# Reordering the transfers and sums where an MLP kernel turns from its up to its down projection

## The reference, cut to what matters

```python
    hm = _rms(x, norm_mlp) @ w_up
    x = x + jnp.square(jax.nn.relu(hm)) @ w_down
...
    y_prompt = _rms(xp, norm_final)
```

## Time and profile before

| | |
|---|---|
| median of 3 runs | 2661.9 us |
| profiled execution, device time | 2661.59 us |
| its span, first to last instruction | 2659.9 us |
| TensorE busy | 2617.6 us, 98% |
| VectorE busy | 1775.3 us, 67% |
| ScalarE busy | 1017.1 us, 38% |
| POOL busy | 148.0 us, 6% |
| mean granted clock of the TensorE | 0.996 of full |
| moved by DMA | 486.32 MB, mean 183 GB/s |
| time for the turn | about 1934 to 2030 us |

### The profile page before, as it was taken

One profiled execution on the slowest core, in us unless ns is written; L12 is line 12 of the kernel. 1 busy time (PEld: TensorE's weight loads), 2 busy tenths in 40 slices (PEclk: granted clock), 3 DMA queues, 4 the chain that ended last, 5 costly groups with the idle time before them and its releaser, 6 DMA issues.

```text
span 2659.9 us, 48846 instructions
## 1 busy us (share of the span) xinstructions
PE 2617.6 (98%) x20436; PEld 2564.5 (96%) x20436; DVE 1775.3 (67%) x2172; ACT 1017.1 (38%) x1317; POOL 148.0 (6%) x235
## 2 busy tenths in 40 slices
PE   8999999999999999999999999999999999999997
PEld 8989999999999998979999999999999999999997
DVE  7656533343443234257988888888887888888888
ACT  6532211111231122133566556555543333333344
POOL 1100000000000001000011110000010000000000
PEclk9999999999999999999999999999999999999998
DMA  8663222222223436433477777666688666566653
GB/s 284 226 219 99 92 87 89 87 88 87 90 82 125 171 111 251 175 145 132 135 247 242 248 252 237 215 239 220 220 301 305 231 223 207 203 218 235 219 168 107
DMA packets 142666, 486.32 MB, mean 183 GB/s; under 512 B 12672, under 2 KB 18944, under 8 KB 131232
## 3 DMA queue, kind: packets, MB, share of 16 engines
q1 hardware_dynamic: 105616, 293.08, 33.2%
q0 software_dynamic: 36880, 190.79, 19.5%
HBM read 402.96 MB, written 80.86 MB: 182 GB/s over the span
## 4 chain that ended last, share of the span: by engine, by line
PE 94%; DVE 2%; DMA 2%; ACT 1%; issue 1%; SPq 0%; DVEq 0%; ACTq 0%
PE psum_main L1731 39%; PE psum_main L2092 27%; PE psum_side L2092 20%; PE psum_main L1838 3%; DMA unit_raw<-weights 1%; PE psum_main L1946 1%; PE psum_main L2018 1%; PE psum_side L1911 1%; DVE unit_low L1405 1%; PE psum_side L1987 1%; DMA residual<-residual_kept 0%; DMA mem_raw<-mem_t 0%; ACT unit_high L846 0%; DVE residual L1697 0%; PE psum_side L1998 0%
## 5 line engine op out<-in xcount | busy, mean ns | idle before, releaser
L846 ACT ACTIVATE unit_high<-unit_raw 128x1024 fp32r<-128x1024 f32 x384 | 402.3, 1055 | 536.2 <-PE psum_main L2092 155.4
L1731 PE MATMUL psum_main<-inner_a,unit_high 128*128 128x272 f32 x3584 | 599.4, 289 | 0.0
L1405 DVE TENSOR_TENSOR unit_low<-unit_raw,unit_high 128x1024 fp32r<-128x1024 f32 x384 | 469.0, 1222 | 109.1 <-ACT unit_high L846 109.0
L643 ACT ACTIVATE unit_high<-unit_raw 128x1024 fp32r<-128x1024 f32 x226 | 239.2, 1059 | 717.6 <-PE psum_main L1731 662.3
L1731 PEld LDWEIGHTS psum_main<-inner_a,unit_high 128*128 128x128 f32 x3584 | 507.2, 188 | 3.1 <-issue 2.9
L1005 DVE TENSOR_TENSOR unit_low<-unit_raw,unit_high 128x1024 fp32r<-128x1024 f32 x226 | 276.2, 1224 | 234.5 <-ACT unit_high L643 231.8
L2092 PE MATMUL psum_main<-hidden,unit_high 128*128 128x272 f32 x2048 | 391.9, 290 | 6.1 <-DVE residual L1572 3.2
L2092 PE MATMUL psum_main<-tokens,unit_high 128*128 128x272 f32 x2048 | 388.5, 288 | 3.3 <-DVE hidden L1542 2.3
L1731 PE MATMUL psum_main<-inner_a,unit_low 128*128 128x272 f32 x1792 | 370.0, 287 | 0.0
L2092 PEld LDWEIGHTS psum_main<-hidden,unit_high 128*128 128x128 f32 x2048 | 324.7, 190 | 6.9 <-DVE residual L1572 3.8
L2092 PEld LDWEIGHTS psum_main<-tokens,unit_high 128*128 128x128 f32 x2048 | 321.8, 189 | 4.2 <-DVE hidden L1542 2.9
(11 more groups left out here) (232 smaller groups left out, 3366.7 us busy)
## 6 DMA issues: line engine op xcount, KB each, us to landing
unit_raw<-weights SPq DMA_DIRECT2D x482, 512.0 KB, 4.1
hidden<-hidden_kept POOLq DMA_DIRECT2D x56, 1088.0 KB, 6.5
hidden_kept<-hidden_staged POOLq DMA_DIRECT2D x31, 1904.0 KB, 7.5
unit_sum<-weights SPq DMA_DIRECT2D x63, 512.0 KB, 3.8
residual_kept<-residual POOLq DMA_DIRECT2D x32, 272.0 KB, 5.4
cache_ring_t<-cache_k POOLq DMA_DIRECT2D x8, 1024.0 KB, 8.2
cache_low_a<-cache_v POOLq DMA_DIRECT2D x8, 1024.0 KB, 10.9
cache_ring_a<-cache_k POOLq DMA_DIRECT2D x8, 1024.0 KB, 7.8
```

The costliest lines, as they stand in the source:

```text
L643: act.activation(WHI[:, s, :], RAW[:, s, :], ACT.Copy).then_inc(high_ready, 1)
L846: act.activation(WHI[:, slot, :], raw, ACT.Copy).then_inc(mlp_high, 1)
L1405: dve.tensor_tensor(WLO[:, slot, :], raw, WHI[:, slot, :].bitcast(F32), ALU.subtract) \
L1731: ins = pe.matmul(out, weights_at(w), moving, start=first and n == 0, stop=last and n == len(passes) - 1)
```

## The change

Three edits, all at the turn. On POOL, the load of hidden block 2 (i == 2, and so all behind it) also waits for `mlp_high` 225, which is the high part of w11 of quad 32. On POOL too, the store of quad 30, the wait for its landing and piece 2 of the residual now stand ahead of the wait for `stage_ready` 64 and piece 1. For quads 33 to 36 (`crowded`), SP loads w11 first, behind its wait for `sum_4` of the quad before, and then w22 and w21, both behind the wait for the fifth low part; w12 and the second w22 follow as before. On the DVE, `sum_1` of these quads stands behind `add_down` of product 4 and the first low part, instead of ahead of them.

```diff
--- before.py
+++ after.py
@@ -410,6 +410,8 @@
             def into(q, tile):
                 return tile if q < QUADS else tile.rearrange("p (u n) -> p u n", u=2)
 
+            crowded = range(QUADS + 1, QUADS + 5)
+
 
             for q in range(2 * QUADS):
                 w11, w12, w21, w22 = blocks(q)
@@ -427,14 +429,18 @@
                     if q == 1:
                         sp.wait_ge(mlp_ready, 5)
                         sp.dma_start(into(q, RAW[:, 2, :]), w21).then_inc(mlp_raw[2], 16)
-                    else:
+                    elif q not in crowded:
                         sp.wait_ge(mlp_ready, PRODUCTS * (q - 1) + 4)
                         sp.dma_start(into(q, SUMW[:, :]), w22).then_inc(mlp_raw[4], 16)
-                    if q > 1:
+                    if q > 1 and q not in crowded:
                         sp.wait_ge(mlp_ready, PRODUCTS * (q - 1) + 5)
                         sp.dma_start(into(q, RAW[:, 2, :]), w21).then_inc(mlp_raw[2], 16)
                     sp.wait_ge(mlp_sum, 4 * q)
                     sp.dma_start(into(q, RAW[:, 0, :]), w11).then_inc(mlp_raw[0], 16)
+                    if q in crowded:
+                        sp.wait_ge(mlp_ready, PRODUCTS * (q - 1) + 5)
+                        sp.dma_start(into(q, SUMW[:, :]), w22).then_inc(mlp_raw[4], 16)
+                        sp.dma_start(into(q, RAW[:, 2, :]), w21).then_inc(mlp_raw[2], 16)
                     sp.wait_ge(mlp_ready, PRODUCTS * (q - 1) + 6)
                     sp.dma_start(into(q, RAW[:, 1, :]), w12).then_inc(mlp_raw[1], 16)
                     if q == 1:
@@ -610,14 +616,16 @@
             last = PRODUCTS * (QUADS - 1)
             for i in range(PRODUCTS):
                 pool.wait_ge(mlp_used, last + i // 2 + 1)
+                if i == 2:
+                    pool.wait_ge(mlp_high, PRODUCTS * QUADS + 1)
                 if i >= 2:
                     landed(0, i - 2)
                 load_hidden(0, i)
-            pool.wait_ge(stage_ready, 2 * QUADS)
-            bring_back(1, 4, 9)
             store_hidden(QUADS - 2)
             pool.wait_ge(hid_stored, 16 * (QUADS - 1))
             bring_back(2, 9, KT)
+            pool.wait_ge(stage_ready, 2 * QUADS)
+            bring_back(1, 4, 9)
             store_hidden(QUADS - 1)
 
 
@@ -1653,7 +1662,7 @@
                     low(q, 6)
                 if tail:
                     low_hidden(n, 1)
-                if q + 1 < 2 * QUADS:
+                if q + 1 < 2 * QUADS and q + 1 not in crowded:
                     sum_1(q + 1)
                 if q == 1:
                     scale_squared()
@@ -1664,6 +1673,8 @@
                     add_down(q, 4, 1, 1, chain(q), ALU.subtract)
                 if q + 1 < 2 * QUADS:
                     low(q + 1, 0)
+                if q + 1 in crowded:
+                    sum_1(q + 1)
 
                 if up:
                     read_up(q, 5, 3, S[:, 2, 0:HALF], PARTIAL[:, 1, :], 2, 1)
```

## The result

The changed kernel takes 2666.93 us (median of 14 runs, 2664.69 to 2669.06), the kernel before 2660.77 us (14 runs on the same chip, 2658.2 to 2662.88). The ratio is 1.0021, with a 95% interval of 1.0014 to 1.0028. The forecast was 2660.5 us, the range 2654.5 to 2666.5. The chance of slower by over 0.2% had been put at 0.14.

The account below looks back on a forecast made before the run. The turn was taken as bound by transfers. From 2661.6 us, -5.6 (start) +8.3 +1.6 (tiles, clock) -2.4 (quad 34) -3.5 (quad 35) +0.5 (later stream) = -1.1 gave 2660.5 us, range 2654.5 to 2666.5.

Parts of the forecast that it names:

- Part 1: Start of quad 32: w11 lands at 1946.6, two TensorE waits and the lower clock go, 5.6 us gained.
- The 1.5 us for the clock: Behind the 2.90 us wait at quad 32: the 1.2 GHz level over 1957 to 1960 goes, 1.5 us gained.
- Part 2: Quad 33: tiles 4 to 8 land at 1987.3, costing 8.3 us plus 1.6 for the clock; quad 34 gains 2.4.
- Rival (b): Quad 33: its weights, squeezed by the store, land at 1978 to 1983 and hold the turn: 2658 us, chance 0.13.
- the waits of quad 34 go: Quad 34: with POOL relieved, weights land near 1999 and waits of 0.94 and 1.41 us go, 2.4 us gained.
- Part 3: Quads 33 to 36: w11 first and sum 1 later gain 3.5 us, the later weight stream costs 0.5.
- The gain of 3.5 us: Product 6 of quad 34: its 1.75 us wait and 1.7 us at the lower clock go.
- The price: Quads 35 and 36: later weight stream costs 0 to 2 us each, taken as 0.5 us in all.
- w12's landing at T + 22 and its need at T + 20: Quad starting at T: w12 lands between T + 15.5 and T + 22, needed by T + 20.
- a sign of being wrong: Quads 34 to 36: TensorE waits for low parts there would show the forecast wrong.
- (d): Later stream at full price: w12 at T + 22 in two quads, 2 us each, one clock drop: 2665.6, chance 0.11.
- (c): Quad 33: tiles come one after the other, landing at 1994.3, product 2 at 1995.2: 2667.5 us, chance 0.14.

Follow-up runs that it names:

- e1: Kernel before plus only POOL's wait of hidden block 2 for the high part of quad 32's w11: 2660.17 us, ratio 0.9996.
- e4: Changed kernel with all three edits, but residual tiles 4 to 8 ahead of store 30's landing wait and tiles 9 to 15: 2664.83 us, ratio 1.0016.
- e8: Kernel before plus POOL's wait and early store 30, with tiles 4 to 8 ahead of tiles 9 to 15; weights and sums as before: 2659.63 us.
- e3: Kernel before plus only the SP and DVE edit (w11 first, sum 1 late) in quads 33 to 36: 2667.91 us, ratio 1.0028.
- e5: Changed kernel without the SP and DVE edit, so both POOL edits on the kernel before: 2664.43 us, ratio 1.0013.
- e10: Kernel before plus the SP and DVE edit moved to quads 41 to 44, where no residual tile moves: 2667.08 us, ratio 1.0021.
- e2: Kernel before plus only POOL's new order, store 30 and tiles 9 to 15 ahead of tiles 4 to 8: 2660.28 us, ratio 0.9998.
- e13: e10 with POOL's hidden block issued after product 3 of quads 40 to 43 now waiting for product 5: 2660.88 us, ratio 1.0003.
- e9: Kernel before plus POOL's wait for w11, and store 31 held until the high part of quad 34's w12 is made: 2655.82 us, ratio 0.9981.
- e12: Kernel before plus only SP's half (w11 first, then w22 and w21) in quads 41 to 44: 2668.63 us, ratio 1.003.
- e14: Kernel before plus only the DVE's half (sum 1 late) in quads 41 to 44: 2659.11 us, ratio 1.0.
- e6: Kernel before plus only the DVE's half (sum 1 late) in quads 33 to 36: 2664.01 us, ratio 1.001.
- e7: Kernel before plus only SP's half (w11 first, then w22 and w21) in quads 33 to 36: 2669.44 us, ratio 1.0031.
- e11: Kernel before plus the SP and DVE edit for quad 35 alone: 2663.14 us, ratio 1.001.

## Why the prediction was wrong, step by step

**Part 1** was right in kind, and in size for the two waits. w11 landed at 1949.7, 2.2 us later than forecast for a turn that begins 0.94 us later, and still in time. Both waits and the low clock went. The 1.5 us for the clock are not in every execution, though (see the last section). Left out was that the rest of the turn is bound by transfers and waits itself when it is reached earlier: e1 keeps 3.3 us of the 5.6 in the profiled execution and 0.7 by the medians.

**Part 2** had the right mechanism and terms that were too small. The store went at 1963.32 (forecast 1961 + 0.9) and took 14.0 us (11). The tiles needed 13.3 us from the first issue (14.7). They landed at 1991.08, 3 us after the forecast, and product 2 started 5.4 us later than before instead of 2.6. The low clock behind it cost 6 x 0.50 = 3.0 us, not 1.6. Rival (b) was true at the same time: w12 of quad 33, with w12 of quad 35 below it,

```profile
unit_raw<-weights SPq DMA_DIRECT2D x1, 512.0 KB, 14.2
...
unit_raw<-weights SPq DMA_DIRECT2D x1, 512.0 KB, 10.1
```

took 14.2 us from 1966.39, landed at 1980.61, within the 1978 to 1983 of (b), and held product 1 for 5.24 us. With 7.15 us of work behind it, it alone would have held product 2 until 1987.8; the tiles moved it on to 1991.88. I had treated the two as alternatives. They hold the same quad, so mending one (e4, e8) shows the other. That the waits of quad 34 go was right.

**Part 3** is the step that failed: it was forecast to gain 3.5 - 0.5 = 3.0 us, and no run shows a gain. Alone it costs 7.1 us (e3), added to e8 4.8 (e4), added to e5 2.2 (the changed kernel: +6.2 against +3.9, which the intervals don't tell apart), and in the quiet quads 5.5 (e10). Both of its terms were wrong.

The gain of 3.5 us was put down to this edit, but the wait ahead of product 6 of quad 34 is gone in e1, e2, e5 and e8 too, which don't have it. Whatever moved POOL's transfers at the turn took that wait away, so beside the two POOL edits nothing was left for the third to gain there.

The price was taken at 0.5 us out of a range of 0 to 4, with the reason that one hidden block at a time leaves room. e10 refutes that: the quiet quads have just that one block, and 5.5 us are lost. I bounded w12's landing at T + 22 and its need at T + 20, and then took a value near the other end without looking which hidden block is issued in the midst of the stream. In e10 the sequence was: w11 at 2141.92, w12 at 2144.62, the block at 2146.01. In the changed kernel quad 34 starts at T = 2010.0, a hidden block is in flight from 2020.18 to 2028.85, quad 35's w12 is issued at 2022.37 and lands at T + 22.5, and quad 35 waits 0.65 + 1.43 = 2.1 us. The 0.65 us are the wait for a low part in quads 34 to 36 that the prediction had named as a sign of being wrong.

**The sum** with the terms as the trace has them: -5.6 (part 1) + 11.0 (tiles: 8.3 + 2.7) + 3.0 (clock) - 5.9 (quads 34 and 35) + 2.1 (later stream) = +4.6, and 0.9 ahead of the turn makes 5.5; the spans differ by 5.6. The excess over the forecast is 2.7 for the tiles, 1.4 for the clock and 1.6 for the stream, so by this count more of the miss lies in part 2 than in part 3. It counts the 3.5 us of quad 34 as a gain of the change, whichever edit made it. The runs count by edit: parts 1 and 2 were forecast at -5.6 + 8.3 + 1.6 - 2.4 = +1.9 and measured +3.9 (e5), part 3 at -3.0 and measured +2.2 beside them.

The measured time lies between rivals (d), 2665.6, and (c), 2667.5, and is neither. The tiles didn't land at 1994.3 as in (c), and w12 was late in one quad and not two, with no drop of the clock, unlike (d). What came was the forecast's late tiles and the late w12 of (b) together, and the later stream on top.

The rule of the Trainium skill (DMA: Bandwidth & Descriptors, Queues, rings and completion order), that each DMA engine takes turns between its queues by the packet, was cited against the change. Beyond the packet counts of rows 4 the traces show no turns, but they show the sharing: with POOL's queue full, a block of 512 KB took 14.2 us here, and that of quad 41 took 10.4 in e10 and 7.7 in e13, where the hidden block beside it was moved. Such sharing deserved more than the 0.13 of rival (b), since it acts in part 3 as well.

## What to carry to other kernels

Where a turn is bound by transfers, count for each one who waits for it and when. Store 31 and the first block of the next chunk had no one waiting, and the kernel that holds those back besides the first edit (e9) is 5.7 us faster than before, where moving the transfers that someone waits for lost 6.2. Two edits that each can't be told from no change can harm each other when one sets the start of the other (e1, e2 and e5: -0.7, -0.6, +3.9). When a load is moved later within a fixed cycle, look what its last part now falls together with, and test the edit in a quiet stretch too, which separates the order from the crowd. Before a gain is put down to one of several edits, see whether the others take the same wait away.

## What was not expected

Executions of the same code differ by small waits. e10, e12, e13 and e14 are the kernel before up to quad 40, but between 2060 and 2130 their profiled executions show waits (of over 0.3 us) of 0.93, 0.87 and 0.83 us (e10), of 0.58 and 0.59 (e12), of 1.15 and 0.69 (e13) and none (e14), where the kernel before had none. They end with a residual addition. e9 has six of 0.4 to 1.2 us between 2000 and 2115. The runs of one kernel spread over 3 to 11 us, and a profiled execution can be 2 to 3 us from the median (e6: 2661.1 in the profile, 2664.0 in the median; e9: 2658.1 and 2655.8). A trace says where a wait is and what ends it; what an edit is worth is read from the medians.

The clock doesn't go by the length of the wait alone. Taken over all traces, the 6 us behind a wait of the TensorE in or behind the turn have a mean granted clock of 1.00 after every wait of up to 1.57 us, and of 0.50 to 0.74 after 21 waits of 1.75 to 7.23 us. But after five others, of 2.79 to 3.33 us, it is 1.00. All five are the wait ahead of quad 32. Ten kernels are the same up to there: before, e2, e3, e6, e7 and e10 to e14. Their wait is 2.78 to 3.33 us; behind it the clock fell in before, e6, e7, e12 and e13, and it did not in e2, e3, e10, e11 and e14. Here are e3 and, with its wait, e14, against the 0.50 of before:

```profile
1957.00:1960.00 3.00, 3.00 (x27) 3.00 (x26) 3.00 (x3) 1.04 (x4) 0.53 (x1) 1.00 0.94 389
```

```profile
1956.84 0.49 PE L2095 MATMUL psum_main<-hidden,unit_high 128*128 128x272 f32 x2 [3.33 <-DVE unit_low L1405]
...
1957.00:1960.00 3.00, 3.00 (x25) 3.00 (x25) 3.00 (x4) 0.53 (x2) 0.47 (x1) 1.00 0.94 394
```

What decides it for one wait these traces don't show. So the 1.5 us that the prediction gives back for the clock ahead of quad 32 are a gain of some executions and not of others, and what the clock costs in one trace may be worth less in a median.
